# One step of a hybrid decoder trunk on one core: squares of the norm loop issued one block sooner, one projection block moved to the first scan level, and GpSimd's first masks behind VectorE's

## The reference

```python
h = rmsnorm(x) * (1 + scale) + shift            # scale, shift: silu(c) @ w_ada
q, k, v, conv_in, a, b, z, g_a, g_b = split(h @ w_in)
o_att = sliding_window_attention(q, k, v)       # window 128, sinks, relative bias
dq, dk, dv = silu(short_conv(conv_in))
dq, dk = l2norm(dq) / sqrt(128), l2norm(dk)     # per head of 128 columns
o_d, S = gated_delta_rule(dq, dk, dv, decay(a), beta(b), S0)
o_d = rmsnorm(o_d) * silu(z)
merged = sigmoid(g_a) * (o_att @ w_att_out) + sigmoid(g_b) * (o_d @ w_delta_out)
x = x + gate1 * rmsnorm(merged @ w_out)
x = x + gate2 * rmsnorm(peer(x))                # per token and head the best 16 of 16384 experts
```

## Time and profile before

| | us |
|---|---|
| median of 3 runs | 1861.8 |
| lowest and highest | 1859.77, 1861.87 |
| profiled execution, its own time | 1853.47 |
| span of the profile, first to last instruction | 1851.7 |

### The profile page before, as it was taken

How to read it: one execution, slowest core, us unless ns; L and a number is a source line. 1 busy time by engine, 2 the same in 40 slices (tenths; PEclk the granted TensorE clock), 3 DMA queues, 4 the chain that set the end, 5 groups by cost and what they waited for, 6 DMA issues and landing times.

```text
span 1851.7 us, 23298 instructions
## 1 busy us (share of the span) xinstructions
PE 1443.2 (78%) x8331; PEld 689.9 (37%) x8331; DVE 1237.7 (67%) x2798; ACT 711.2 (38%) x1812; POOL 643.2 (35%) x610
## 2 busy tenths in 40 slices
PE   9999989999898879788788766666666666666666
PEld 4777777777455447453233111101111110000001
DVE  3077667676866675777766676777667677667665
ACT  3145563213544543945333322432222252222223
POOL 1100000320443334434344444444444444444442
PEclk9999999999899989789889867866777676676666
DMA  9533472016999999989999999999999999999997
GB/s 359 170 126 113 150 249 76 24 69 226 422 421 420 422 409 409 422 355 413 422 423 420 424 424 424 424 424 424 425 424 423 424 419 415 424 418 424 420 417 315
DMA packets 101347, 648.59 MB, mean 350 GB/s; under 512 B 11890, under 2 KB 12058, under 8 KB 33221
## 3 DMA queue, kind: packets, MB, share of 16 engines
q0 software_dynamic: 76912, 555.82, 72.4%
q1 hardware_dynamic: 24128, 91.20, 13.5%
q10 hardware_dynamic: 192, 0.09, 0.0%
HBM read 641.89 MB, written 6.18 MB: 350 GB/s over the span
## 4 chain that ended last, share of the span: by engine, by line
PE 39%; DMA 38%; DVE 9%; ACT 8%; issue 4%; POOL 1%; SPq 0%; ACTq 0%; DVEq 0%; POOLq 0%
DMA arena<-in_euv,consts 37%; PE abank L959 24%; DVE arena L2438 4%; PE dbank L1712 4%; PE dbank L959 4%; PE fsum L1706 2%; PE fsum L1712 2%; ACT consts L921 1%; ACT L919 1%; ACT L821 1%; ACT small L919 1%; POOL arena L488 1%; DMA arena<-in_wstream 1%; PE fsum L1023 1%; ACT L505 1%
## 5 line engine op out<-in xcount | busy, mean ns | idle before, releaser
L2438 DVE CUSTOM_DVE_ANT_0 arena<-arena 128x1024 f32<-128x1024 f32 x520 | 634.2, 1224 | 407.9 <-DMA arena<-in_euv,consts 406.8
L488 POOL DMA_INDIRECT arena<-in_euv,consts x520 | 583.7, 1122 | 774.3 <-PE dbank L1712 342.2
L959 PE MATMUL abank<-arena 128*128 128x128 f32 (+4 forms) x2520 | 564.8, 382 | 22.5 <-DVE arena L2176 5.1
L1712 PE MATMUL dbank<-arena,consts 128*32 128x512 f32 x1024 | 359.7, 835 | 198.4 <-ACT consts L921 197.5
L959 PEld LDWEIGHTS abank<-arena 128*128 128x128 f32 (+1 forms) x2520 | 405.2, 194 | 177.3 <-issue 64.4
L919 ACT ACTIVATE small<-small 128x1 f32<-128x1 f32 x520 | 104.8, 202 | 637.5 <-DVE small L2438 630.9
L1712 PE MATMUL fsum<-arena,consts 128*32 128x512 f32 x512 | 190.5, 864 | 115.3 <-ACT consts L921 114.8
L1712 PEld LDWEIGHTS dbank<-arena,consts 128*32 128x32 f32 x1024 | 42.1, 123 | 476.1 <-ACT consts L921 462.8
L505 ACT ACTIVATE arena<-abank 128x512 f32<-128x512 f32 (+7 forms) x243 | 117.1, 482 | 248.9 <-PE abank L959 235.6
L921 ACT ACTIVATE consts<-arena,small 128x32 f32<-128x32 f32 x520 | 167.1, 321 | 17.0
L1712 PEld LDWEIGHTS fsum<-arena,consts 128*32 128x32 f32 x512 | 21.5, 125 | 266.4 <-ACT consts L921 263.8
(11 more groups left out here) (336 smaller groups left out, 1207.5 us busy)
## 6 DMA issues: line engine op xcount, KB each, us to landing
arena<-in_wstream SPq DMA_DIRECT2D x142, 512.0 KB, 6.8
arena<-in_euv,consts POOLq DMA_INDIRECT x520, 13.2
arena<-in_wout SPq DMA_DIRECT2D x8, 1024.0 KB, 8.7
arena<-in_x SPq DMA_DIRECT2D x5, 512.0 KB, 6.8
arena<-in_sdel POOLq DMA_DIRECT2D x1, 2048.0 KB, 9.3
out_deltas<-arena POOLq DMA_DIRECT2D x1, 2048.0 KB, 11.8
out_yp<-arena SPq DMA_DIRECT2D x4, 512.0 KB
arena<-mod SPq DMA_DIRECT2D x3, 512.0 KB, 11.9
```

Source lines behind the costliest of these rows:

```text
L488: pool.indirect_dma_start(ring[n % SLOTS], None, I["euv"], bass.IndirectOffsetOnAxis(cur[:, u % 2, c:c + 1], 0)).then_inc(ring_in[n % SLOT ...
L959: return pe.matmul(out, lhsT, rhs, start=first, stop=last)
L1712: last = pe.matmul(out[e][to:to + 32, :], weighed, v, start=h == 0 and kk == 0, stop=h == PH - 1 and kk == 3, skip_group_check=True)
L2438: TTR(uh, uh, rep[j] if t < NT else h2sb, 1.0, 0.0, ALU.mult, ALU.add, dot[:, n // NQ % 2, n % NQ:n % NQ + 1]).then_inc(s.dots_done, 1)
```

## The change

Three edits. First, in VectorE's norm loop the squares of blocks 0 and 1 come ahead of the loop. Iteration m then waits for the root of block m-1, squares block m+1, takes the reciprocal and the multiply of block m-1, and does its small jobs last. Second, the third projection block runs in level 1 behind the second product of chunk 0 on TensorE (and at the matching places on ScalarE and VectorE), in place of level 2. The fourth stays in level 3. Third, GpSimd waits until VectorE has made its four masks of level 1 before it makes its first mask. No instruction that computes is added or removed.

```diff
--- before.py
+++ after.py
@@ -457,6 +457,7 @@
             pool.dma_start(I["mod"], mrow2).then_inc(s.mod_out, 16)
             pool.wait_ge(s.mod_out, 16)
             pool.dma_start(sdel, I["sdel"]).then_inc(s.sdel_in, 16)
+            pool.wait_ge(s.lm_ready, NT)
             for lv in range(1, 6):
                 mask = consts[:, C_LVL + (lv + 1) * P:C_LVL + (lv + 2) * P]
                 for ch in range(NT):
@@ -675,6 +676,8 @@
             for lv in range(1, 6):
                 for ch in range(NT):
                     first_product(ch)
+                    if lv == 1 and ch == 1:
+                        others_attended(N_EARLY)
                 if lv == 1:
                     for pair in range(2):
                         empty(strips[:, pair, :])
@@ -686,8 +689,8 @@
                 if lv == 3:
                     empty(sdv[2], slice(0, 32), func=ACT.Sqrt, bias=eps, scale=1.0 / P)
                     act.sem_inc(s.sa_ready, 1)
-                if 2 <= lv < 2 + B_ATT - N_EARLY:
-                    others_attended(lv - 2 + N_EARLY)
+                if lv == 3:
+                    others_attended(B_ATT - 1)
 
             def mixed(t, e):
                 if t < NT:
@@ -1354,6 +1357,8 @@
                 for ch in range(1, NT):
                     first_product(lv, ch)
                     second_product(lv, ch - 1)
+                    if lv == 1 and ch == 1:
+                        attended()
                 samples(lv)
                 if lv >= 4:
                     for g in range(2):
@@ -1956,10 +1961,20 @@
             step(TT(gtmp, nat[:, :, 256:260], bc(cols[:, K_DT:K_DT + 4], 1, NT + 1), ALU.add), s.gx_ready)
             q0 = prob[0:64, 0, 0:P]
             mx, nm, sm_, es, sink = mx8[0:64, 0:1], nm8[0:64, 0:1], sm8[0:64, 0:1], es8[0:64, 0:1], cols[0:64, K_SINKS:K_SINKS + 1]
-            for m in range(2 * DH + 1):
-                if m < 2 * DH:
-                    dve.wait_ge(s.silu_out, m + 1)
-                    step(TT(sqb[:, m % 2, :], ct[:, m, :], ct[:, m, :], ALU.mult), s.sq_ready)
+            def squared(m):
+
+                dve.wait_ge(s.silu_out, m + 1)
+                step(TT(sqb[:, m % 2, :], ct[:, m, :], ct[:, m, :], ALU.mult), s.sq_ready)
+
+            squared(0)
+            squared(1)
+            for m in range(1, 2 * DH + 1):
+                dve.wait_ge(s.rn_ready, m)
+                if m + 1 < 2 * DH:
+                    squared(m + 1)
+                r = rnb[:, (m - 1) % 2, :]
+                step(recip(r, r))
+                step(TT(ct[:, m - 1, :], ct[:, m - 1, :], r, ALU.mult), s.l2_done)
                 if m in (1, 2, 4, 5):
                     for c in range(*{1: (4, 6), 2: (6, 8), 4: (8, 10), 5: (10, 12)}[m]):
                         modulation(c)
@@ -1978,11 +1993,6 @@
                     step(TT(sm_, sm_, es, ALU.add))
                     step(recip(sm_, sm_))
                     step(TS(q0, q0, sm_, None, ALU.mult), s.prob_ready)
-                if m >= 1:
-                    dve.wait_ge(s.rn_ready, m)
-                    r = rnb[:, (m - 1) % 2, :]
-                    step(recip(r, r))
-                    step(TT(ct[:, m - 1, :], ct[:, m - 1, :], r, ALU.mult), s.l2_done)
             dring.n += 4 * DH + 2
             step.n[s.dring_free.name] += 4 * DH + 2
 
@@ -2132,11 +2142,13 @@
                 for ch in range(NT):
                     if ch == NT - 1:
                         sampled(lv)
-                        if 2 <= lv < 2 + B_ATT - N_EARLY:
-                            attended(lv - 2 + N_EARLY)
+                        if lv == 3:
+                            attended(B_ATT - 1)
                     b = dring.to_read()
                     step(TT(Tc[:, ch, :], Tc[:, ch, :], b[:, :], ALU.subtract), s.dring_free)
                     merged_transpose(lv, ch)
+                    if lv == 1 and ch == 0:
+                        attended(N_EARLY)
                 if lv == 1:
                     state_answers()
```

## The result

| | us |
|---|---|
| before, median of 11 runs | 1862.2 (1859.8 to 1867.4) |
| after, median of 11 runs | 1855.2 (1846.6 to 1856.9) |
| ratio, 95% interval | 0.9947 (0.9936 to 0.9959) |
| profiled execution of after, its own time and its span | 1855.9, 1854.0 |

The ratio isn't the quotient of the two medians, which lie 7.0 us apart. 1851.6 was forecast, with 1848.0 to 1858.3 as the range. The two profiled executions alone would tell the opposite: the one of before took 1853.5 us, the one of after 1855.9. That contradiction is the main thing to explain.

The account below looks back on a forecast made before the run. The prediction took a chain through TensorE, ScalarE and VectorE to bound the kernel before the first gather, and bytes after it. Norm loop -4.3, block -5.9 and wait 0 made -10.2 us: 1861.8 to 1851.6, range 1848.0 to 1858.3.

Parts of the forecast that it names:

- A: Norm loop: issuing squares sooner and small jobs last brings the key transposes from 284.9 to 280.6 us, -4.3 us.
- B: Third projection block: moving it saves 7.05 us in scan level 2 and costs 1.2 in level 1, -5.9 us.
- C: GpSimd's wait in level 1: hidden behind TensorE's moved block, taken as 0 us, bounds 0 and -1.7.
- The step that failed: Front before the first gather: time saved there starts the gathers sooner and comes off the end one for one.
- The bound of -1.7: GpSimd's wait in level 1: most it could give, the 1.7 us lost by VectorE's stretched mask and merge.
- a case without worth: GpSimd's masks might still meet VectorE's operations in this or a later level, leaving the wait at zero; no chance given.
- The first step of the prediction: Gather stage: everything after the first gather at 459 us is bound by bytes, read from 900 to 1300 us.
- The give-back rival: Gather stage: its start moves by 10 us and its end doesn't, giving 1858.5 to 1863 us; chance 8%.
- The clock rival: Ahead of the scan levels' products: a new hole lowers TensorE's clock; 15 us at it gives 1866.6 us; chance 5%.

Follow-up runs that it names:

- e9: Changed kernel with the norm loop as before, so block move and GpSimd's wait only; 1854.7 us, ratio 0.9960 to before.
- e2: Kernel before with only the third projection block moved from scan level 2 to level 1; 1857.6 us, ratio 0.9974 to before.
- e3: Kernel before with only GpSimd's wait for VectorE's four masks of level 1; 1859.1 us, ratio 0.9983 to before.
- e4: Changed kernel without GpSimd's wait, so norm loop and block move only; 1856.2 us, ratio 0.9957 to before.
- e6: Kernel before with only the norm loop's new order, second series on another chip; 1860.6 us, ratio 0.9993 to before.
- e8: Changed kernel, GpSimd also holding the last level's masks until VectorE's last transpose of level 4; 1853.5 us, ratio 0.9944 to before.
- e12: Changed kernel with GpSimd's extra wait for the last level's masks, run once more; 1852.9 us, ratio 0.9951 to before.
- e1: Kernel before with only the norm loop's new order, first series; 1861.7 us, ratio 1.0000 to before.
- e7: Changed kernel unchanged, run again in a second series on another chip; 1856.4 us, ratio 0.9966 to before.
- e10: Kernel before with one level 3 product issued eleven times, 8.9 us of TensorE work added ahead of the gathers; 1871.7 us, ratio 1.0055.
- e11: Changed kernel with a small unused matmul behind each weighed sum of gather units 1 to 11; 1874.3 us, ratio 1.0067 to before.
- e5: Kernel before, unchanged, profiled and timed again on another chip; 1863.4 us, ratio 1.0003.

## Why the prediction was right, and where its steps were not

**Total.** -10.2 us were forecast on a base of 1861.8. The two series gave -9.9 and -6.3 (1862 x 0.0034); their mean is -8.1. At C0 it was -9.5. That the first series came so near to the forecast is in part luck: A, priced at 4.3, shows 0.7 to 3.2 at the end, and B and C without it (e9) show 7.4 where 5.9 was priced. The choice to subtract from the median of the runs, and not from the profiled execution, was right: that execution had the shortest C0 to C14 of the table (633.9).

**Norm loop.** The chain was as forecast: no wait for a square in blocks 5 and 6, VectorE's last multiply over at 278.9 (forecast 278.4). The transposes were forecast at 280.6. In the eight profiles with the new loop they came at 280.2 to 283.3 (mean 281.8), in the six without it at 284.4 to 286.1 (mean 285.4), so 3.6 us sooner where 4.3 was priced. Much of the scatter is TensorE's clock, at two places. One is at 245 us, ahead of the waits that the change takes away: the granted clock from 245.0 to 249.2 was 0.50 to 0.63 in eight profiles (after, e2, e3, e4, e6, e8, e9, e12) and 1.00 in the six others. The row of after:

```profile
245.00:249.20 4.20, 4.20 (x30) 1.85 (x29) 0.56 (x1) 3.03 (x5) 0.00 (x0) 0.59 0.12 23
```

The other is the wait of 2.08 us ahead of the decays (1.8 in the prediction), a hole that the change opens. Behind it the clock stayed up in after, e1 and e7 and was low in e8 and e12, and T is 283.2 and 283.3 there. First after, then e8:

```profile
268.50:276.50 8.00, 5.44 (x43) 5.19 (x43) 7.69 (x8) 6.87 (x11) 0.58 (x1) 1.00 0.74 279
```

```profile
268.50:276.50 8.00, 7.28 (x32) 6.93 (x33) 7.34 (x8) 6.13 (x10) 0.58 (x1) 0.57 0.75 279
```

The step that failed is the next one: "Time saved there should start the gathers sooner and come off the end one for one". For A, three comparisons say -0.7 (mean of e1 and e6), -0.7 (change against e9) and -3.2 us (e4 against e2), where -4.3 was priced. Each has an interval of about 2 to 3 us to each side (the second also compares different chips). Together, by an estimate from these intervals, they allow up to some 2.5 us, and not the 3.8 of C0. For 9 us of added work e10 shows two thirds at least to arrive. Why less of A arrives isn't settled. In the profiles C0 to C14 is 644.5 us on the mean of seven executions with the new loop and 641.2 of six without it (e11 left out, as it adds work there), a difference of the right size, but smaller than what two executions of one program differ by.

**Block.** Right in each term: level 1 longer by 1.27 us (1.2 forecast), level 2 shorter by 7.05, nothing late behind it. With the block in level 1 it is 50.04 to 50.06 us from the transposes to the states in all eight profiles that have it there; without the block and the wait it is 48.5 to 49.8, as the clock behind the hole of 3.89 us varies. -5.9 was forecast, and T to C0 in e9 is 167.8 in place of 173.7, so 5.9 shorter. In the change it is 168.7, 5.0 shorter. The other 0.9 us is the clock in the fifth level: behind the hole of 2.49 us it fell in the change and not in the two profiles of the kernel before, where the same hole is there. Before first, then after:

```profile
384.20:388.20 4.00, 3.88 (x21) 2.55 (x21) 3.69 (x10) 0.60 (x1) 1.26 (x1) 1.00 0.02 4
```

```profile
375.00:379.20 4.20, 4.10 (x18) 3.77 (x19) 3.04 (x7) 0.60 (x1) 1.26 (x1) 0.61 0.01 4
```

**GpSimd's wait.** 0 on top of B, as taken. The bound of -1.7 is what it gives the first level alone: 1.72 us in e3. What the prediction left out is the same collision in level 5, which it named only as a case without worth: there nothing covers VectorE, and the wait of e8 is worth 1.9 us of the front. The Trainium skill, SBUF — State Buffer, section SBUF: two separate sides, says that a VectorE operation with two SBUF inputs and a GpSimd operation that reads SBUF take a shared port pair in turn, each for its whole length. The trace agrees in direction (e3); an operation of 0.69 us became 0.78 to 0.95 us longer.

**The gather stage.** The first step of the prediction, that everything after the first gather is bound by bytes, doesn't hold for the first part, some 640 of 1400 us, as e11 shows. It was read from a table of 900 to 1300 us and laid over 459 to 1850. A table of 498 to 898 of before would have shown what the one of after above shows: TensorE busy 85% of the time (338.5 of 400), clock 0.92, 410 GB/s in place of 423. The DMA share alone wouldn't have told, as it is 1.00 there. The give-back rival reasoned that the length isn't rigid. That was so, but it varies by several us between executions of one program, and e10 shows no shortening when C0 comes later (640.0). Between profiles the same part of the stage shows the variation: TensorE gets 334 instructions done in before, 241 in e1. First before (from C0 + 184 us), then e1 (from the same distance):

```profile
642.60:700.60 58.00, 46.38 (x334) 26.75 (x332) 37.06 (x86) 26.85 (x59) 17.54 (x18) 0.91 1.01 405
```

```profile
639.80:697.80 58.00, 42.47 (x241) 21.42 (x242) 33.97 (x83) 28.95 (x60) 20.55 (x19) 0.85 0.94 360
```

**The clock rival.** It didn't decide, but it was there: a hole of 2.5 us cost 0.9 us in the profile of after, 2.9 in e2 (T to C0 170.8 in place of the 167.9 that 173.7 and the block's -5.8 make), as much in e11 (170.9), and nothing in the profile of before. The other hole, of 2.08 us, is new with the change, and e8 and e12 reached T 1.6 us later than after did.

**What stays open.** Where some 3 us of the norm loop's gain go. The runs exclude that the front doesn't keep it (C0 is sooner by 3.8 and 4.2 us) and that half of any shift is swallowed (e10). They don't exclude a smaller loss that all shifts share. With spreads of 8 to 11 us in C0 to C14 from one execution to the next, single profiles can't name the place, and timed runs of this number tell 2 to 3 us apart at best.

## What to carry to other kernels

Look at each stage's table before calling it bound by one thing: a row from the middle of a stage says nothing of its first third. Price a change of the front from the front's own marks, subtract it from the median of the runs, and don't compare the spans of single profiles when a later stage varies by more than the change is worth. Where two engines' SBUF operations collide, first ask whether a longer matmul covers the delay: here such a wait was worth nothing in the covered level and 1.9 us in the uncovered one. Where the profile says that a wait ended with an engine whose result was ready long before, look for the last result that arrived.

## What the runs showed of the hardware

- A GpSimd operation on SBUF beside a VectorE operation with two SBUF inputs stretches both: VectorE 0.69 to 1.47 or 1.64 us, and 1.42 to 3.33 for two; two GpSimd masks 2.50 to 2.94. VectorE operations with a PSUM input, such as the one at 373.56 beside the third mask, kept their 0.69.
- A hole of 2.49 or 2.50 us stands ahead of the same product (x8) of level 5 in twelve of the fourteen profiles. The product took 1.13 or 1.14 us in six of them (before, e5, e6, e9, e2, e11), 1.57 in e4, 1.75 in e10, and 2.04 or 2.05 in four (after, e7, e1, e3). In e2 and e11 the slow stretch came right behind it (7.60 and 7.23 us for the next 20, 4.05 in e6). So the same hole left the clock at 2.4 GHz in four executions and was followed by 1.2 GHz, at once or a product later, in the others, of one program too (e1 and e6). No rule for it came out of these rows.
- The first 630 us of the gathers took between 633.9 and 650.0 us for kernels with the same work there, the last 760 us between 758.2 and 760.0.
